# The ten norms of a two-block transformer: eight buffers for the squares, the root's table fetched first, scale and shift on ACT

## The reference

```
def _rms_norm(x, g):
    return x * rsqrt(mean(x * x, axis=-1) + 1e-6) * g

# first block: six norms without a shift
f = _swiglu(_rmsnorm(x, ffn1_pre_g), ...)            # norm n1
x = x + 0.5 * _rmsnorm(f, ffn1_post_g)               # norm p1
h = _rmsnorm(x, mix_pre_g)                           # norm n2
...                                                  # two attentions, gates, w_out
x = x + _rmsnorm(merged @ w_out, mix_post_g)         # norm p2
f = _swiglu(_rmsnorm(x, ffn2_pre_g), ...)            # norm n3
x = x + 0.5 * _rmsnorm(f, ffn2_post_g)               # norm p4

# second block, twice: two norms with scale and shift
h = _rms_norm(x, norm1_g) * (1.0 + sc1) + sh1        # norm l1
...                                                  # four mixers on h @ w_in
x = x + g1 * (y @ w_out)
h = _rms_norm(x, norm2_g) * (1.0 + sc2) + sh2        # norm l2
x = x + g2 * _conv_glu_ffn(h, ...)
```

## Time and profile before

| engine | busy us | share of the span |
|---|---|---|
| PE matmul | 2673.7 | 91% |
| PE weight load | 2131.1 | 73% |
| ACT | 1124.6 | 38% |
| POOL | 1093.1 | 37% |
| DVE | 1019.0 | 35% |

### The profile page before, as it was taken

One profiled execution on the slowest core, in us unless ns is written; L12 is line 12 of the kernel. 1 busy time (PEld: TensorE's weight loads), 2 busy tenths in 40 slices (PEclk: granted clock), 3 DMA queues, 4 the chain that ended last, 5 costly groups with the idle time before them and its releaser, 6 DMA issues.

```text
span 2928.8 us, 51928 instructions
## 1 busy us (share of the span) xinstructions
PE 2673.7 (91%) x16576; PEld 2131.1 (73%) x16576; DVE 1019.0 (35%) x1760; ACT 1124.6 (38%) x1631; POOL 1093.1 (37%) x570
## 2 busy tenths in 40 slices
PE   6999979997997999987999879999989998799998
PEld 5888857686875888865677567777766875677776
DVE  3334131213214444113745533431037554333310
ACT  4443233324433444223433525552244244355521
POOL 2444424545442444432331224444423212244433
PEclk9999989999997999997998889999989987899999
DMA  5555313211321656322210023332322100233232
GB/s 188 186 197 187 121 56 122 85 62 33 98 90 53 220 177 202 95 71 96 76 45 3 9 65 93 93 93 86 99 95 73 38 3 16 65 87 99 86 91 81
DMA packets 78125, 273.46 MB, mean 93 GB/s; under 512 B 8592, under 2 KB 9360, under 8 KB 77840
## 3 DMA queue, kind: packets, MB, share of 16 engines
q1 hardware_dynamic: 77968, 271.40, 29.2%
HBM read 269.26 MB, written 2.10 MB: 93 GB/s over the span
## 4 chain that ended last, share of the span: by engine, by line
PE 84%; DVE 5%; ACT 4%; issue 4%; POOL 2%; DMA 1%; DVEq 0%; ACTq 0%; SPq 0%; POOLq 0%
PE bank L268 22%; PE bank L269 22%; PE bank L270 22%; PE bank L1415 4%; PE bank L1666 3%; POOL w_lo L255 1%; DVE tmp L348 1%; PE bank L315 1%; ACT tmp L306 1%; PE bank L712 1%; PE bank L1689 1%; PE bank L436 1%; PE bank L714 1%; PE bank L713 1%; PE bank L1268 1%
## 5 line engine op out<-in xcount | busy, mean ns | idle before, releaser
L255 POOL TENSOR_TENSOR w_lo<-raw,w_hi 128x1024 fp32r<-128x1024 f32 (+2 forms) x406 | 946.7, 2332 | 1521.8 <-PE bank L270 1070.2
L268 PE MATMUL bank<-h_hi,w_hi 128*128 128x512 f32 x2112 | 840.8, 398 | 68.7 <-DVE tmp L351 21.3
L269 PE MATMUL bank<-h_lo,w_hi 128*128 128x512 f32 x2112 | 832.4, 394 | 0.0
L270 PE MATMUL bank<-h_hi,w_lo 128*128 128x512 f32 x2112 | 831.4, 394 | 0.0
L246 ACT ACTIVATE w_hi<-raw 128x1024 fp32r<-128x1024 f32 x408 | 427.3, 1055 | 482.2 <-PE bank L270 441.8
L268 PEld LDWEIGHTS bank<-h_hi,w_hi 128*128 128x128 f32 x2112 | 402.5, 191 | 181.3 <-issue 82.9
L270 PEld LDWEIGHTS bank<-h_hi,w_lo 128*128 128x128 f32 x2112 | 402.8, 191 | 86.2
L269 PEld LDWEIGHTS bank<-h_lo,w_hi 128*128 128x128 f32 x2112 | 403.4, 191 | 82.2 <-issue 0.5
L268 PE MATMUL bank<-hidden_hi,w_hi 128*128 128x512 f32 x704 | 279.6, 397 | 5.3 <-POOL w_lo L255 5.3
L269 PE MATMUL bank<-hidden_lo,w_hi 128*128 128x512 f32 x704 | 279.4, 397 | 0.0
L270 PE MATMUL bank<-hidden_hi,w_lo 128*128 128x512 f32 x704 | 279.1, 396 | 0.0
(11 more groups left out here) (395 smaller groups left out, 3070.9 us busy)
## 6 DMA issues: line engine op xcount, KB each, us to landing
ada<-in_ada SPq DMA_DIRECT2D x96, 512.0 KB, 4.5
raw<-in_ff_up SPq DMA_DIRECT2D x88, 512.0 KB, 5.7
raw<-in_l.ff_up SPq DMA_DIRECT2D x88, 512.0 KB, 3.6
raw<-in_l_fm SPq DMA_DIRECT2D x36, 512.0 KB, 3.7
raw<-in_ff_down SPq DMA_DIRECT2D x32, 512.0 KB, 3.6
raw<-in_l.ff_down SPq DMA_DIRECT2D x32, 512.0 KB, 3.6
raw<-in_l_wo SPq DMA_DIRECT2D x16, 512.0 KB, 3.7
raw<-in_ff_down SPq DMA_DIRECT2D x16, 384.0 KB, 3.1
```

Of the source, the lines that this page charges most:

```text
L255: pool.tensor_tensor(self.wlo[lo][:, 0:kt * P], self.raw[slot][:, 0:kt * P], self.whi[slot][:, 0:kt * P].bitcast(F32), ALU.subtract).then_ ...
L268: pe.matmul(bank[:, :], wh[:, b], hi[:, k, :], start=first, stop=False)
L269: pe.matmul(bank[:, :], wh[:, b], lo[:, k, :], start=False, stop=False)
L270: return pe.matmul(bank[:, :], wl[:, b], hi[:, k, :], start=False, stop=last)
```

## The change

Three edits, in the ten norms:

1. `rms_act` writes the eight squares to eight tiles of their own, and no longer waits for PE's sums between them. `rms_pe` reads them there. For p1, p2 and p4 `ready` becomes `max(k - 4, 0)`: tiles 0 to 4 wait for the first output of the last pass, tiles 5, 6 and 7 for the second, third and fourth.
2. Before the first square ACT takes the root of one constant column, so the root's table set is loaded there.
3. For l1 and l2, `shifted_dve` and `shifted_act` take the place of `pre_dve` and `pre_act`: DVE multiplies `x` by bank 6 alone; ACT applies gain and shift twice, once with rounding to `h_hi` and once without, in place; DVE subtracts.

```
-            if k >= 2:
-                m.held(act.wait_ge(*m.done(f"{nm}.sum{k - 2}")))
-            act.activation(self.tmp[k % 2][:, :], src[:, k, :], ACT.Square).then_inc(*m.mark("act", f"{nm}.sq{k}"))
+            if k == 0:
+                act.activation(self.tmp[2][:, 0:1], self.eps, ACT.Sqrt).then_inc(*m.mark("act", f"{nm}.table"))
+            act.activation(sq[:, k, :], src[:, k, :], ACT.Square).then_inc(*m.mark("act", f"{nm}.sq{k}"))
...
+    def shifted_dve(self, dve, nm):
+        m = self.m
+        self.rms_dve(dve, nm)
+        for k in range(KD + 2):
+            t = self.tmp[4 + k % 4]
+            if k < KD:
+                if k >= 4:
+                    m.held(dve.wait_ge(*m.done(f"{nm}.h{k - 4}")))
+                dve.tensor_tensor(t[:, :], self.x[:, k, :], self.bank[6][:, :], ALU.mult).then_inc(*m.mark("dve", f"{nm}.v{k}"))
+            if k >= 2:
+                m.held(dve.wait_ge(*m.done(f"{nm}.u{k - 2}")))
+                dve.tensor_tensor(self.hl[:, k - 2, :], self.tmp[4 + (k - 2) % 4][:, :], self.hh[:, k - 2, :].bitcast(F32), ALU.subtract).then_inc(*m.mark("dve", f"{nm}.h{k - 2}"))
+
+    def shifted_act(self, act, nm, gain, shift):
+        m = self.m
+        for k in range(KD):
+            t = self.tmp[4 + k % 4]
+            m.held(act.wait_ge(*m.done(f"{nm}.v{k}")))
+            act.activation(self.hh[:, k, :], t[:, :], ACT.Identity, scale=gain(k), bias=shift(k)).then_inc(*m.mark("act", f"{nm}.hh{k}"))
+            act.activation(t[:, :], t[:, :], ACT.Identity, scale=gain(k), bias=shift(k)).then_inc(*m.mark("act", f"{nm}.u{k}"))
...
-            mc.pre_dve(dve, "l1", lambda k: self.gain[:, k:k + 1], lambda k: self.mod[:, k:k + 1])
+            mc.shifted_dve(dve, "l1")
+            m.held(dve.wait_ge(*m.mine("dve")))
...
-            mc.rms_act(act, "l2", mc.x, lambda k: f"l.wo.out{k}")
-            mc.pre_act(act, "l2")
+            mc.rms_act(act, "l2", mc.x, lambda k: f"l.wo.out{k}", self.squares)
+            mc.shifted_act(act, "l2", lambda k: self.gain[:, 8 + k:9 + k], lambda k: self.mod[:, 24 + k:25 + k])
...
-            mc.rms_act(act, "p1", mc.f, lambda k: f"ff1.f{k % 4}")
+            mc.rms_act(act, "p1", mc.f, lambda k: f"ff1.f{max(k - 4, 0)}")
```

More of the change, by code:

```diff
@@ L187, in __init__ @@
         self.f = self.alias("f", [P, KD, T], F32, self.places["h_lo"])
+        self.sq = self.alias("h_squares", [P, KD, T], F32, self.places["h_hi"])
     def sbuf(self, name, shape, dt=F32):
@@ L296, in pe_two, with rms_act @@
         ins.then_inc(self.chunk_done, 1)
-    def rms_act(self, act, nm, src, ready):
-        m = self.m
+    def rms_act(self, act, nm, src, ready, sq=None):
+        m, sq = self.m, self.sq if sq is None else sq
         for k in range(KD):
@@ L303, in rms_act, with rms_pe @@
                 m.held(act.wait_ge(*m.done(ready(k))))
-            if k >= 2:
-                m.held(act.wait_ge(*m.done(f"{nm}.sum{k - 2}")))
-            act.activation(self.tmp[k % 2][:, :], src[:, k, :], ACT.Square).then_inc(*m.mark("act", f"{nm}.sq{k}"))
+            if k == 0:
+                act.activation(self.tmp[2][:, 0:1], self.eps, ACT.Sqrt).then_inc(*m.mark("act", f"{nm}.table"))
+            act.activation(sq[:, k, :], src[:, k, :], ACT.Square).then_inc(*m.mark("act", f"{nm}.sq{k}"))
         m.held(act.wait_ge(*m.done(f"{nm}.sum{KD - 1}")))
         act.activation(self.tmp[2][:, 0:P], self.bank[7][:, 0:P], ACT.Sqrt, bias=self.eps, scale=1.0 / D).then_inc(*m.mark("act", f"{nm}.std"))
-    def rms_pe(self, pe, nm):
-        m = self.m
+    def rms_pe(self, pe, nm, sq=None):
+        m, sq = self.m, self.sq if sq is None else sq
         for k in range(KD):
@@ L314, in rms_pe @@
             for t in range(NT):
-                x = pe.matmul(self.bank[7][32 * t:32 * t + 32, 0:P], self.ones[:, 0:32], by_time(self.tmp[k % 2], t),
+                x = pe.matmul(self.bank[7][32 * t:32 * t + 32, 0:P], self.ones[:, 0:32], by_time(sq[:, k, :], t),
                               start=k == 0, stop=k == KD - 1)
@@ L339, in post_dve, with pre_dve @@
         m.held(dve.wait_ge(*m.mine("dve")))
-    def pre_dve(self, dve, nm, gain, shift=None, source=lambda x: x, target=lambda x: x):
+    def pre_dve(self, dve, nm, gain, source=lambda x: x, target=lambda x: x):
         m = self.m
@@ L347, in pre_dve @@
                 t = self.tmp[4 + k % 4]
[L348 to L351, removed]
+                dve.scalar_tensor_tensor(t[:, :], self.x[:, k, :], gain(k), self.bank[6][:, :], ALU.mult, ALU.mult).then_inc(*m.mark("dve", f"{nm}.u{k}"))
             if k >= 2:
@@ L1115, in dve_all @@
             mc.run(dve, self.s_o, wo)
-            mc.pre_dve(dve, "l2", lambda k: self.gain[:, 8 + k:9 + k], lambda k: self.mod[:, 24 + k:25 + k])
+            mc.shifted_dve(dve, "l2")
+            m.held(dve.wait_ge(*m.mine("dve")))
             self.ff.dve(dve, l)
@@ L1903, in act_all @@
             mc.rms_act(act, "l1", mc.x, None)
-            mc.pre_act(act, "l1")
+            mc.shifted_act(act, "l1", lambda k: self.gain[:, k:k + 1], lambda k: self.mod[:, k:k + 1])
             m.held(act.wait_ge(*m.done("l.mu1")))
@@ L1936, in pe_all @@
             mc.run(pe, self.s_o, wo)
-            mc.rms_pe(pe, "l2")
+            mc.rms_pe(pe, "l2", self.squares)
             self.ff.pe(pe, l)
@@ L2144, in act_first @@
             pw_out.act(act)
-            mc.rms_act(act, "p2", mc.f, lambda k: f"wo.out{k % 4}")
+            mc.rms_act(act, "p2", mc.f, lambda k: f"wo.out{max(k - 4, 0)}")
             mc.rms_act(act, "n3", mc.x, lambda k: f"p2.x{k}")
@@ L2148, in act_first @@
             ff2.act(act)
-            mc.rms_act(act, "p4", mc.f, lambda k: f"ff2.f{k % 4}")
+            mc.rms_act(act, "p4", mc.f, lambda k: f"ff2.f{max(k - 4, 0)}")
         def dve_first(dve):
@@ L2154, in dve_first @@
             mc.post_dve(dve, "p1", lambda k: col("ffn1_post_g", k), 0.5)
[L2155 removed]
+            mc.pre_dve(dve, "n2", lambda k: col("mix_pre_g", k), grid_order, block_order)
             pa_kq.dve(dve)
```

1 line of the change is left out of this document (removed).

## The result

| kernel | runs, us | median |
|---|---|---|
| before, beside it | 2929.96, 2922.33, 2926.64, 2923.46 | 2925.05 |
| after | 2868.91, 2869.96, 2879.65, 2877.20 | 2873.58 |

The ratio is 0.9828 with a 95% interval of 0.9813 to 0.9842: 50.3 us less. Forecast were 44.3 us less, 2882 us, and a range from 2874, so the median lies 8.4 us under the forecast and 0.4 us under the range's low end. The profiled execution took 2868.91 us (span 2867.0), 61.9 us less than the profiled one of before.

What follows compares the result with a forecast made beforehand. PE bounds the long products; the norms take bare time. Terms 9.6 + 7.6 + 7.9 + 19.2 = 44.3 us less gave 2882 us against the median 2926.64; own range 2874 to 2890, wider range 2874 to 2897.

Steps and rivals of the forecast that it cites:

- root behind the last copy, p1, p2, p4: Norms p1, p2, p4: root starts 3.2 us earlier (bounds 1.6 and 3.3), 9.6 us for three.
- root, l1 of layer 0: Norm l1: one table load instead of two, root at 1328.65 against 1332.47, 3.8 us; 7.6 for two.
- root behind the last output, l2: Norm l2: root at 1722.03 against 1725.99, 3.95 us (lower bound 2.6); 7.9 for two.
- ACT's step: Norms l1, l2: one scale-and-shift instruction on ACT every 0.69 us, bounds 0.51 and 0.80.
- last subtraction: DVE in l1, l2: ends at T + 12.8 against T + 17.62, 4.8 us (bounds 3.1, 5.5); four times, 19.2.
- T: The first multiplication of a norm's h on DVE, from which later times in that norm are counted.
- PE's start of l2, its last tile: After l2: PE starts at T + 5.35, against T + 10.54; last tile's matmuls at T + 12.95, against T + 17.79.
- root to T: In the norms: from root to the first multiplication of h, 3.82 us, untouched by the change.
- rival B: Norms: sums don't pack and ACT's instructions don't overlap; only 28 us gained, 2898 us; chance 0.12.
- A: After l2: PE starts late from its loop jump or code fetch, still T + 10.54; 2892 us; chance 0.08.
- C: Behind the norms: gain given back in weight stream or layers' constants, under 8.8 us left, 2918 us and more; chance 0.05.
- D: Norms l1, l2: ACT's two instructions are dear, slower from a 1.43 us step on; 2949 us at 1.8; chance 0.03.

Runs made afterwards that it cites:

- late_table: The changed kernel without the early small root, so the root's table loads behind the last square; 2883.33 us, ratio 0.9853 to the kernel before.
- busy_before: The kernel before with 8 (p1, p2, p4) or 6 (other norms) unused matmuls on PE between last sum and spread; 2915.45 us, ratio 0.9978.
- last_pass: The changed kernel with the old rule k % 4 for the tile a square waits for in p1, p2, p4; 2886.11 us, ratio 0.9887 to the kernel before.
- four_marks: The changed kernel with four one-element marked copies on DVE behind norm l2; 2881.83 us, ratio 0.9866 to the kernel before.
- fused: The changed kernel with l1, l2 redivided: DVE multiplies by gain too and adds shift while subtracting, ACT shifts and rounds once; 2866.34 us, ratio 0.9807 to before.

## Why the prediction was right, and where it was not

| step | forecast | measured |
|---|---|---|
| root behind the last copy, p1, p2, p4 | 1.97 us, gain 3.2 | 1.89 to 1.91, gain 3.3 |
| root, l1 of layer 0 | gain 3.8 | 3.95 |
| root behind the last output, l2 | 2.23 us, gain 3.95 | 2.21, gain 3.98 |
| ACT's step | 0.69 us | 0.706 |
| last subtraction | T + 12.8 | T + 13.05 |
| third chunk behind l1 | T + 17.4 | T + 17.69 |
| PE's start of l2, its last tile | T + 5.35, T + 12.95 | T + 5.38, T + 13.19 |
| root to T in p1, p2, p4, l1, l2 | "untouched" | 0.92 us less each |

**Squares.** The sum by the rows is 3 x 3.3 + 2 x 3.95 + 2 x 3.98 = 25.8 us, forecast 25.1 (the second layer gave 3.8 and 4.2). The eight sums pack (2.16 us for 64 records), which rival B denied.

**Scale and shift.** 4 x 4.6 = 18.4 us, forecast 19.2. That the two misses nearly cancel is luck. The measured step is 0.706 and the end T + 13.05, where I had 0.69 and T + 12.8. The Trainium skill's formula ("ScalarE: Activation LUTs", section "What ACT_TABLE_LOAD costs") gave a step of 0.706 and T + 13.1, and the trace agrees with it. On the second rule of that section of the Trainium skill, some 1.4 us of draining at each switch of tables, `late_table` sides with the rows: the root starts 1.29 us behind the load's start.

**The step that failed** is "From root to T are 3.82 us, untouched". I had priced that piece at nothing, because the change touches no instruction there. It holds PE's spread, and PE's clock hangs on what PE did just before. Seven times 0.92 is 6.4 us. The evidence lay in the trace: the prediction itself used 0.23 and 0.46 us for one matmul at the two levels, and counted the low clock in l1 and l2, yet not at the spread. `busy_before` shows the cause, `last_pass` shows it from the other side. The missed 6.4 us are also why the median came out just under the low end of my range.

Less standing alone does not explain it: `late_table` has the short spread in l2 behind the same 3.03 us of standing as before, since the sums came without gaps. The gaps alone don't explain it either: `busy_before` kept them, filled most of the standing, and got 1.13 to 1.16 us. Both are part of what PE did just before.

With it the sum is 25.8 + 18.4 + 6.4 = 50.6 us, against 50.3 by the ratio. The other 11 of the 61.9 us between the two profiled executions are the stretches: 5.9 from n2 to p2, 2.8 in the two layers' mixers (1.2 more in the first, 4.0 less in the second), 1.6 between the layers, and the rest at the two ends. Had I compared those two executions alone, I would have looked in the change for 11 us that the next two profiles don't show.

**The rivals.** A fell by the start at T + 5.38 and by `four_marks`. B fell by the 2.16 us and by ACT's 0.706. C: counted in the timeline, T to the 145th matmul is 4.6 to 4.8 us shorter in l1 and in l2 of both layers, so nothing was given back, and the product from n1's 145th matmul to p1's last copy took 330.34 us before and 330.35 after. D: the step is half of the 1.43 us that it needed.

## What to carry to other kernels

When a wait on PE gets shorter, price the small matmuls behind it anew: they may run at the higher granted clock, and that gain is in none of the lines that changed. A wait with `back=1` in a loop's first pass names a mark by its place in a count, so each instruction added or removed ahead of the loop moves it; count it through. And take at least two profiles of one kernel before explaining a stretch whose instructions are the same.

## What the runs showed of the hardware that I had not expected

Eight sums whose data are ready take 2.16 us at the high clock (0.27 each) and 3.23 us with the low clock at their start (l1), where a lone one takes 0.47. Standing still alone does not decide the clock: after the same 1.55 us of it the spread took 1.16 us where PE had been busy without a break (changed kernel, p1) and 2.08 us where the sums had come with gaps (`last_pass`), and after the same 3.03 us it took 1.13 (`late_table`, l2) and 2.05 (kernel before, l2). It has its part: in `late_table` some 2.3 us behind unbroken sums gave 1.72, 1.29 and 2.07 us in p1, p2 and p4, where some 1.5 gave 1.16 each time. And a DVE operation that waits for the one before it to end starts 0.72 us behind a plain subtraction (n2) and 0.89 behind one with a shift (`fused`), where a neighbour without such a wait starts 0.67 behind.
